# The first pair of feed-forward rows by plain products, in a one-core decoder step with Strassen products

## The reference

```python
def residual_block(x, mix, w_out_l, g_ffn, wg, wu, wd):
    x = x + mix @ w_out_l
    h = rmsnorm(x, g_ffn)
    return x + (jax.nn.silu(h @ wg) * (h @ wu)) @ wd
```

## Time and profile before

| | |
|---|---|
| median of 3 executions | 3206.66 us (3204.07 to 3212.55) |
| the profiled execution | 3213.07 us |
| its span in the trace | 3211.4 us |
| mean granted TensorE clock | 0.951 of full |
| TensorE busy | 2994.2 us |
| VectorE busy | 2013.2 us |
| ScalarE busy | 879.9 us |
| GpSimd busy | 695.3 us |
| DMA | 340.08 MB, mean 106 GB/s |

### The profile page before, as it was taken

One profiled execution on the slowest core, in us unless ns is written; L12 is line 12 of the kernel. 1 busy time (PEld: TensorE's weight loads), 2 busy tenths in 40 slices (PEclk: granted clock), 3 DMA queues, 4 the chain that ended last, 5 costly groups with the idle time before them and its releaser, 6 DMA issues.

```text
span 3211.4 us, 58867 instructions
## 1 busy us (share of the span) xinstructions
PE 2994.2 (93%) x22932; PEld 2774.9 (86%) x22932; DVE 2013.2 (63%) x3427; ACT 879.9 (27%) x1507; POOL 695.3 (22%) x774
## 2 busy tenths in 40 slices
PE   7899988999889999999989999889897999999997
PEld 6699975868789999999977999667687999999997
DVE  5798996696554444554348989865956544445444
ACT  3422123243233333300123122123323333332001
POOL 4153300001133333200041542000002333331000
PEclk9999989699899999999989999897998999999999
DMA  7354434142112222422142443352310222223222
GB/s 261 101 158 125 137 113 190 74 135 103 33 49 78 76 79 80 145 91 87 48 146 84 146 146 133 134 200 78 123 61 27 80 80 74 81 75 125 90 87 99
DMA packets 128646, 340.08 MB, mean 106 GB/s; under 512 B 20278, under 2 KB 71623, under 8 KB 123383
## 3 DMA queue, kind: packets, MB, share of 16 engines
q1 hardware_dynamic: 79426, 177.19, 15.4%
q0 software_dynamic: 33088, 102.84, 10.5%
q10 hardware_dynamic: 15844, 56.18, 5.1%
HBM read 266.10 MB, written 74.53 MB: 106 GB/s over the span
## 4 chain that ended last, share of the span: by engine, by line
PE 69%; DVE 20%; issue 4%; ACT 2%; DMA 2%; DVEq 1%; POOLq 1%; POOL 0%; SPq 0%; ACTq 0%
PE PS L1454 27%; PE PS L1476 15%; DVE U L2292 10%; PE PS L1068 7%; PE PS L1296 2%; PE PS L1403 2%; PE PS L1405 2%; PE PS L1404 2%; PE PS L1082 2%; PE PS L992 1%; PE PS L913 1%; PE PS L1014 1%; PE PS L1033 1%; DVE U L2381 1%; DVE U L2398 1%
## 5 line engine op out<-in xcount | busy, mean ns | idle before, releaser
L2292 DVE TENSOR_SCALAR_CACHE_REDUCE U<-U,smu 32x2080 bf16<-32x2080 f32 (+6 forms) x462 | 504.7, 1146 | 13.7 <-issue 1.8
L1454 PE MATMUL PS<-XAR,RGR 128*128 128x264 f32 x3168 | 404.6, 290 | 40.2 <-ACT XAR L1535 31.8
L1454 PEld LDWEIGHTS PS<-XAR,RGR 128*128 128x128 f32 x3168 | 400.9, 193 | 42.7 <-issue 33.2
L2180 DVE TENSOR_TENSOR RGR<-WS,RGR 128x512 fp32r<-128x512 f32 x308 | 238.2, 775 | 288.5 <-ACT RGR L1535 287.8
L1454 PE MATMUL PS<-XBR,RGR 128*128 128x264 f32 x2816 | 409.8, 287 | 8.5 <-DVE RGR L2180 8.5
L1454 PEld LDWEIGHTS PS<-XBR,RGR 128*128 128x128 f32 x2816 | 371.8, 190 | 8.9 <-DVE RGR L2180 8.9
L583 POOL DMA_DIRECT2D WS<-wjobs x176 | 94.6, 538 | 1191.5 <-PE PS L1476 492.3
L1535 ACT ACTIVATE U<-PS 128x528 f32<-128x528 f32 (+12 forms) x338 | 166.1, 502 | 568.6 <-PE PS L1454 253.7
L645 POOL TENSOR_TENSOR WS<-WS 128x512 f32<-128x512 f32 x176 | 257.2, 1467 | 151.7 <-DVE RGR L2180 65.3
L1535 ACT ACTIVATE RGR<-WS 128x512 fp32r<-128x512 f32 x308 | 193.0, 628 | 276.9 <-PE PS L1454 276.9
L1454 PE MATMUL PS<-HnR,RGR 128*128 128x264 f32 x1408 | 229.5, 285 | 0.0
(11 more groups left out here) (322 smaller groups left out, 5313.8 us busy)
## 6 DMA issues: line engine op xcount, KB each, us to landing
WS<-wjobs POOLq DMA_DIRECT2D x113, 512.0 KB, 3.9
WS<-wjobs ACTq DMA_DIRECT2D x50, 512.0 KB, 4.6
hmid<-U SPq DMA_DIRECT2D x44, 528.0 KB, 2.6
WS<-wjobs POOLq DMA_DIRECT2D x48, 384.0 KB, 3.3
Hn<-ckT SPq DMA_DIRECT2D x16, 896.0 KB, 10.7
Hn<-hmid SPq DMA_DIRECT2D x4, 3168.0 KB, 11.5
U<-kT_pool SPq DMA_DIRECT2D x160, 64.0 KB, 2.0
xres<-U SPq DMA_DIRECT2D x2, 4224.0 KB, 16.5
```

The lines of the kernel that those rows point to most:

```text
L1454: m = mm(out, w[:, k * P:(k + 1) * P], x[:, k, t], start=fresh and n == 0 and k == 0, stop=n == 2 and k == 3, skip_group_check=True)
L2180: tt(out=lo, in0=plain(p, i, g), in1=hi.bitcast(F32), op=ALU.subtract).then_inc(wp_lo, 1)
L2292: ts(U[0:m, JUNK[i]:JUNK[i] + w // 2].bitcast(BF16), s, CANDF[0:m, i:i + 1], None, op, ALU.add, accum_out=into[0:m, i:i + 1])
```

## The change

Pair 0 of each layer is no longer done by Strassen's scheme but by plain products; the scheme starts with pair 1.

- **TensorE:** `first_pair` takes the place of `gate_up(0)`. For each of the four weight tiles n (gate, up, gate, up) and each half of the tokens it adds up 2 (feature halves, `part`) x 2 (z) x 3 (passes) x 4 (feature blocks) = 48 matmuls of 264 columns in the two banks 2n and 2n + 1: 384 in all. The order is by what they need: the first half of the tokens, high by high on the first two blocks of b11 for tiles 0 to 2, then on the next two, tile 3, then the low weights, then the low part of b11, then b21; after that the second half of the tokens (b12, b22) by tiles 0 and 1, tile 2, tile 3.
- **Weights of pair 0:** whole tiles of 128x1024 are split at once: `row_high` (ACT; two while the last squares are formed, the third after the norm's inverse, the fourth after b11), `row_low` (DVE), which writes the low part into the tile's own slot. So a slot is in use until TensorE is done with the tile: `slot_used` for the loads of pair 1 now waits for the end of tile k on TensorE (`un_ps`, `NUNIT + 5 + k`) and not for `wp_lo`.
- **Activations:** `row_scale` works on half of the tokens at a time, the first half of the tokens first; it starts when two thirds of the inverse root are there. b11's high part is copied in two pieces. The sums t1, t2, t3 and t4 are formed by DVE alone, later in the list; t1, t3 and t4 get their high parts from ACT after the last product of `first_pair` and in the first steps of pair 1, and their low parts from `late_low` on DVE after steps 1, 3 and 5 of pair 1.
- **POOL:** the weights' sums of pair 0, `high_sums` and `high_low` go.
- **Evictions of pair 0:** four silu of 128x528 by ACT (`first_silu`) and four multiplications by DVE (`first_hidden`), straight from PSUM; the 6 snapshots and 6 additions of a Strassen pair are gone for pair 0.

The core of the diff, TensorE, POOL and the weights' side:

```diff
-                return wp_lo, W_LO + 14 * p + 11 + k
+                return (wp_lo, W_LO + 14 * p + 11 + k) if p else (un_ps, NUNIT + 5 + k)
...
+        X_ITEMS = ("b11a", "b11b", "b21", "b12", "b22", "t2", "t1", "t3", "t4")
+        X_LOWS = ("b11", "b21", "b12", "b22", "t2", "t1", "t3", "t4")
...
+        def row_hi(n):
+
+            o = (n + 2) % 3 * 1024
+            return RGR[:, o:o + 1024] if n < 3 else split_cols(XHI[3], 1024)
+
+        def row_lo(n):
+            return WSR[:, (J_GU + n) % NSLOT, 0:1024]
...
                 for p in range(NPAIR):
-                    weight_sums(L, p)
+                    if p:
+                        weight_sums(L, p)
                     for j in range(J_GU + 4 * p + 4, J_GU + 4 * p + 8):
                         load(j, job_floats(j), j - NSLOT)
...
+            def first_pair():
+
+                def products(n, half, part, w, x, ks=range(4)):
+                    hi, lo = x_part(half, part)
+                    ww, xx = (row_hi, row_lo)[w](n), (hi, lo)[x]
+                    first, last = part == 0 and w == 0 and x == 0, part == 1 and w == 1
+                    for z in range(2):
+                        for k in ks:
+                            m = mm(PS[:, 2 * n + z, 0:TQ], ww[:, (4 * part + k) * P:(4 * part + k + 1) * P],
+                                   xx[:, k, z * TQ:(z + 1) * TQ], start=first and k == 0, stop=last and k == 3,
+                                   skip_group_check=True)
+                    return m
+
+                for n, ks in ((0, (0, 1)), (1, (0, 1)), (2, (0, 1)), (0, (2, 3)), (1, (2, 3)), (2, (2, 3)),
+                              (3, (0, 1)), (3, (2, 3))):
+                    pe.wait_ge(wp_hi, row_hi_done(n))
+                    pe.wait_ge(x_hi, X_HI + ks[0] // 2 + 1)
+                    products(n, 0, 0, 0, 0, ks)
+                for n in range(4):
+                    pe.wait_ge(wp_lo, row_lo_done(n))
+                    products(n, 0, 0, 1, 0)
+                pe.wait_ge(x_lo, lo_done("b11"))
+                for n in range(4):
+                    products(n, 0, 0, 0, 1)
+                for n in range(4):
+                    pe.wait_ge(x_hi, hi_done("b21"))
+                    products(n, 0, 1, 0, 0)
+                    pe.wait_ge(x_lo, lo_done("b21"))
+                    products(n, 0, 1, 0, 1)
+                    products(n, 0, 1, 1, 0).then_inc(un_ps, 1)
+                for group in ((0, 1), (2,), (3,)):
+                    for part in range(2):
+                        for n in group:
+                            if part == 0:
+                                pe.wait_ge((f_silu, f_mul)[n % 2], n // 2 + 1)
+                            pe.wait_ge(x_hi, hi_done(("b12", "b22")[part]))
+                            products(n, 1, part, 0, 0)
+                            pe.wait_ge(x_lo, lo_done(("b12", "b22")[part]))
+                            products(n, 1, part, 0, 1)
+                            m = products(n, 1, part, 1, 0)
+                            if part:
+                                m.then_inc(un_ps, 1 if n < 3 else 7)
```

ACT's list after the squares, and DVE's `norm_split`:

```diff
                 norm_inverse(0)
-                for i in range(2):
-                    x_copy(i)
+                row_high(L, 2)
+                x_copy("b11a")
+                x_copy("b11b")
+                row_high(L, 3)
+                x_copy("b21")
                 table(ACT.Silu, 5)
-                for p in range(NPAIR):
+                x_copy("b12")
+                first_silu(0, 0)
+                x_copy("b22")
+                first_silu(0, 1)
+                x_copy("t2")
+                first_silu(1, 0)
+                weight_high(L, 14)
+                weight_high(L, 15)
+                first_silu(1, 1)
+                weight_high(L, 16)
+                x_copy("t1")
+                for p in range(1, NPAIR):
                     gates(L, p)
...
+                v.wait_ge(nrm_inv, 2)
+                for q in range(4):
+                    i = row_scale(q, 0)
+                    if q % 2:
+                        i.then_inc(fx_row, 1)
+                row_low(2)
+                low("b11", x_low(0), b11, x_high(0))
+                row_low(3)
+                for q in range(4, 8):
+                    i = row_scale(q, 0)
+                i.then_inc(fx_row, 1)
                 v.wait_ge(nrm_inv, NCH)
                 for q in range(4):
-                    i = row_scale(q)
+                    i = row_scale(q, 1)
                 i.then_inc(fx_row, 1)
...
+                low("b21", x_low(1), b21, x_high(1))
+                for q in range(4, 8):
+                    i = row_scale(q, 1)
                 i.then_inc(fx_row, 1)
...
+                low("b12", x_high(6), b12, x_high(4))
+                first_hidden(0, 0)
+                v.drain()
+                tt(out=b11, in0=b12, in1=b11, op=ALU.subtract)
                 v.drain()
                 tt(out=t2, in0=b22, in1=b11, op=ALU.subtract).then_inc(fx_sum, 1)
...
+                tt(out=b12, in0=b22, in1=b12, op=ALU.subtract).then_inc(fx_sum, 1)
+                v.wait_ge(fx_sum, 2)
+                low("b22", x_low(5), b22, x_high(5))
+                first_hidden(0, 1)
                 tt(out=b21, in0=b21, in1=t2, op=ALU.subtract).then_inc(fx_sum, 1)
...
+                low("t2", x_low(2), t2, x_high(2))
+                first_hidden(1, 0)
+                weight_low(14)
+                weight_low(15)
+                weight_low(16)
+                first_hidden(1, 1)
```

More of the change, by code:

```diff
@@ L458, in plain, with hi_done, lo_done, row_hi_done @@
                     first[:, 512:1024], second[:, 512:1024])[i]
+        X_ITEMS = ("b11a", "b11b", "b21", "b12", "b22", "t2", "t1", "t3", "t4")
+        X_LOWS = ("b11", "b21", "b12", "b22", "t2", "t1", "t3", "t4")
+        OPERAND = ("b11", "b21", "t2", "t1", "t3", "b22", "t4")
+        NX_HI, NX_LO = len(X_ITEMS), len(X_LOWS)
+        def hi_done(name):
+            return X_HI + X_ITEMS.index("b11b" if name == "b11" else name) + 1
+        def lo_done(name):
+            return X_LO + X_LOWS.index(name) + 1
+        def row_hi(n):
[3 more added lines that the diff above has]
+            return WSR[:, (J_GU + n) % NSLOT, 0:1024]
+        def row_hi_done(n):
+            return W_HI + (n + 1 if n < 3 else 14)
+        def row_lo_done(n):
+            return W_LO + (n + 1 if n < 3 else 14)
+        def x_part(half, part):
+            if half == 0:
+                return x_high(part), x_low(part)
+            return (x_high(5), x_low(5)) if part else (x_high(4), x_high(6))
         def ring(q):
@@ L1521, in _ @@
                 norm_sums(0)
-                for p in range(NPAIR):
+                first_pair()
+                for p in range(1, NPAIR):
                     gate_up(p)
@@ L2144, in norm_split @@
+                row_low(2)
[4 more added lines that the diff above has]
+                i.then_inc(fx_row, 1)
                 v.wait_ge(nrm_inv, NCH)
                 for q in range(4):
-                    i = row_scale(q)
+                    i = row_scale(q, 1)
                 i.then_inc(fx_row, 1)
-                for q in range(4, 6):
-                    row_scale(q)
-                low(0, b11)
@@ L2151, in norm_split @@
-                for q in range(6, 8):
-                    i = row_scale(q)
+                low("b21", x_low(1), b21, x_high(1))
+                for q in range(4, 8):
+                    i = row_scale(q, 1)
                 i.then_inc(fx_row, 1)
-                tt(out=b11, in0=b12, in1=b11, op=ALU.subtract).then_inc(fx_sum, 1)
-                low(1, b21)
-                weight_low(3)
+                low("b12", x_high(6), b12, x_high(4))
+                first_hidden(0, 0)
+                v.drain()
@@ L2162, in norm_split @@
-                weight_low(4)
-                low(3, b11)
-                gated(0, 2)
-                weight_low(5)
-                v.wait_ge(fx_pool, 1)
-                low(5, b22)
-                gated(0, 3)
-                weight_low(6)
-                gated(0, 4)
-                low(6, b21)
+                v.wait_ge(fx_sum, 3)
+                low("t2", x_low(2), t2, x_high(2))
[3 more added lines that the diff above has]
+                weight_low(16)
@@ L2458, in add_out @@
                     if m == KR - 2:
-                        for q in range(3):
-                            weight_low(q)
+                        for n in range(2):
+                            row_low(n)
                 gather_last(0, NCH - 1)
@@ L2740, in _ @@
                 norm_split(L)
-                for p in range(NPAIR):
+                for p in range(1, NPAIR):
                     for n in range(14):
-                        if p == 0 and n <= 4:
-                            if n == 4:
-                                weight_low(7)
-                            continue
                         gated(p, n)
                         weight_low(14 * p + n + 3)
+                        if p == 1 and n in (1, 3, 5):
```

(1 more changed line is left out.)

134 lines of the change are left out of this document (69 added, 65 removed).

## The result

| | before | after |
|---|---|---|
| median of 6 executions | 3205.82 us (3199.80 to 3212.55) | 3175.23 us (3166.86 to 3178.67) |
| profiled execution | 3213.07 us | 3177.38 us |
| its span | 3211.4 us | 3175.6 us |
| mean granted TensorE clock | 0.951 | 0.958 |

The ratio is 0.9896 with a 95% interval of 0.9885 to 0.9907: 33 us less (30 to 37), where 39.6 were forecast; the two medians of the table differ by 30.6. The change is faster, and the measured median lies in the range of 8 in 10 (3156 to 3186), but above the forecast's own (3160 to 3173); the forecast's own ratio, 3167 / 3206.7 = 0.9876, lies just outside the interval.

A forecast was written before the change was run, and what follows sets the result against it. TensorE was taken as the bound, with waits and cold clock in pair 0. Start 7.8, waits 11.6, cold spells 5.4, less 5.9 for matmuls, rest 0.9: 19.8 us per layer, 39.6 twice, giving 3167 us; 8-in-10 range 3156 to 3186.

The forecast's parts named there:

- When TensorE starts: Start of the first pair: TensorE's first matmul comes at 862.6 instead of 870.4 us.
- Whether it stays busy: Inside the first pair: every operand comes before TensorE needs it, so the pair ends at 912.2 us.
- The closest place: VectorE's low part of b22 in the first pair: ready at 893.0, wanted at 895.6, slack 2.6 us.
- The cold time: Start of the first pair: one spell of 5.4 us at half pace, costing 2.7 us; two of three spells gone.
- The pair: Output projection's end to the first pair's end: 912.2 for 932.0 us, 19.8 us less per layer.
- My split of the gain into start, waits and clock: First pair, per layer: start 7.8 us earlier, waits 11.6 and cold spells 5.4 gone, 48 matmuls 5.9 more.
- VectorE's sums: Sums on VectorE in the first pair: 2.34 us each with GpSimd idle, where the rows show 6.94 and 3.25.
- The first rival: VectorE's sums in the first pair stay long by themselves: 5.6 us per layer, 3178 us; 8 in 100.
- Whether pair 1 is ready: Behind the first pair: step 18's weights have 3.9 us of slack, late high and low parts fit; costed at nothing.
- the second rival: Pair 1's weights are late through a slow fourth load and sums: 6.8 us per layer, 3181 us; 7 in 100.
- Nothing is lost behind: Stages after the first pair: no new wait appears; the rival that nothing is gained, 3207 us, had 3 in 100.
- The slower rival: Clock stays low through the first pair's small matmul groups: 24.4 us per layer lost, 3255 us; 2 in 100.

The follow-up runs named there:

- e_more: The changed kernel with 48 more matmuls in the first pair of each layer; ratio to the kernel before 0.9936, pair 64.58 and 64.60 us.
- e_late: The changed kernel with the early start undone: VectorE waits for the inverse root's last third and scales b12 before b11; ratio to the kernel before 0.9912.
- e_warm: The changed kernel with 48 unneeded matmuls in TensorE's wait before the pair; ratio to the kernel before 0.9868, pair 56.26 and 56.24 us.
- b_half: The kernel before with only the half rows and early start, Strassen kept for pair 0; ratio to the kernel before 1.0012.
- b_dve: The kernel before with only t3 and its low part moved from GpSimd to VectorE, Strassen kept for pair 0; ratio to the kernel before 0.9976.
- e_low: The changed kernel with t1's low part moved before step 17's low weights on VectorE; ratio to the kernel before 0.9876, ten pairs 411.17 us.
- three b runs: b_half, b_dve and b_both: the kernel before with one or both parts of the change, Strassen kept for pair 0; ratios 1.0012, 0.9976 and 1.0000.
- e_best: The changed kernel with the edits of e_low and e_warm together; median 3166.53 us, ratio to the kernel before 0.9864.
- b_both: The kernel before with the edits of b_half and b_dve together, Strassen kept for pair 0; ratio to the kernel before 1.0000.

## Why the prediction was right, point by point

- **When TensorE starts.** Forecast 8.9 us after the end of the output projection (853.7 to 862.6), measured 8.9 (852.86 to 861.73). Half rows took 0.70 each and not 0.65, which cost nothing here. The norm's last third did come earlier without GpSimd's sum: the two last additions of squares took 1.17 us, not 2.38.
- **Whether it stays busy.** Right. No wait inside the pair. The closest place was the low part of b22, at 892.4; TensorE used it at about 894.6, so the slack was some 2 us for the 2.6 forecast. That what was added late in the pair counts in full (e_more) and that the start moves the end (e_late, e_warm) bear out that TensorE alone set the end.
- **The cold time.** Right: one spell, 5.5 us from the first matmul. e_warm prices it at 2.4 to 2.5 us per layer, against the 2.7 taken.
- **The pair.** Forecast 19.8 us less, measured 19.72 and 19.55. My split of the gain into start, waits and clock was an account of what stood on TensorE, not of what each edit brings: alone, the early start brought nothing (b_half), and GpSimd's relief 4.7 and 4.6 (b_dve). The parts do not add up, and the code gives a reason: with Strassen's scheme all four quarters and two sums are needed by the third product. The plain products make the early start worth something (e_late), since 192 matmuls need only the first half of the tokens.
- **VectorE's sums.** The first rival is out: t2 took 2.36 us with GpSimd idle. (One reading of the prediction was wrong, at no cost to its sum: the six whole rows that VectorE scales before b11's low part are b11, b12 and half of b21 and of b22.) b_dve (3.49 beside a sum of 1.29) and `late_low` (3.46 beside GpSimd's sums, 2.62 and 2.35 in other places) show the same exclusion. That is the rule of the Trainium skill ("SBUF — State Buffer", "Who interferes with whom"), and the traces agree with it in each of these places.
- **Whether pair 1 is ready: the step that was off.** "I cost all of this at nothing" should have been 1.33 us per layer, 2.7 in all. The two waits of 0.50 and 0.32 us delay the starts behind them by 0.7 and 0.6, because idle time is counted from the end of a matmul, and matmuls overlap: 128 of them start over 16.36 us at 911.27, where 15.7 is the full pace. It was not the late load by itself, the second rival's mechanism, but that rival came near: step 18's low weights were there with 0.5 us to spare where I had 3.9. The fourth load was issued 0.8 us after the pair's end and took 4.9 us to its sum, not 3.8, and 1.15 us lay between that sum and the one for step 18. I had taken the load of an idle queue, and this one had company: the stores of the first pair's hidden rows (528 KB each) go out at the same moments. The two stores are issued at 900.56 and about 912.6. The loads issued beside them, at 900.33 and 912.09, landed after 6.0 and 4.8 us (4.8 for the fourth in the second layer too), the other two after 3.6 and 3.7. That the stores are the cause was not tried. What set the waits in the end was VectorE's list: the low part of t1 stood ahead of step 19's low weights, ran beside GpSimd's sums and took 3.46 us. I had let VectorE's three late low parts fit "between" because each is shorter than a step, and had not placed GpSimd's sums of the same moment beside them, though the prediction itself leans on how the two engines exclude each other. e_low shows it: with the load as late as before, the move takes the 1.33 us away.
- **Nothing is lost behind.** Nearly right. From pair 2 to pair 11 nothing waits. One place stays open, TensorE's one wait in the first down products, for VectorE, which waits for a weight load: 0.7 and 1.0 us before, 1.8 and 1.9 after. In the three b runs it is 0.8 to 1.2, in e_late and e_low 1.8 to 2.0, in e_more and e_best 0.8 to 1.2, in e_warm 1.6 and 1.0. So the changed code does not force the longer wait, but four of its six traces show it and none without the change does; at most 1.9 us of the whole are at stake.
- **The number.** 39.6 us forecast; 36.6 by the stretches, 33 (30 to 37) by the times. 2.7 of the 3 us between the first two are pair 1; the rest between stretches and times is within the interval.
- **The slower rival** (the clock stays low through small groups) is out. From 869 to 911 the matmuls come in groups of 8 whose waits are already met, and the granted clock is 1.00 throughout; the groups of 4 lie in the cold spell, which ended all the same at 867.2. The second failure mode of the Trainium skill ("TensorE: Matmul & The Clock Gate", section "A second HAM failure mode: psum-queue depth-cycling") did not show in this order.

## What to carry to other kernels

A scheme that saves products can be the wrong one for the first piece, when its operands are still being made: here 14% more matmuls on data that is ready beat waiting for sums, and the reordering that feeds them was worth 2.0 us per layer without them. Account for such a stretch by where the bottleneck engine stands still, but don't read the account as a price list of the edits. And when VectorE and GpSimd both work on SBUF, place their lists side by side in time before calling either of them hidden.

## What the runs showed of the hardware that I had not expected

- In TensorE's wait of 6.3 us matmuls that nobody needs kept the granted clock at 1.00: 48 of 264 columns, 6.25 us, saved 2.4 us after it, and the pair's first matmul came no later (8.88 and 8.87 us).
- Halving VectorE's instructions along the free dimension cost little but not nothing: four of 528 elements took 2.80 us, two of 1056 took 2.53, both without a sum of GpSimd beside them. With sixteen halves instead of eight wholes (b_half, b_both) the sum t1 started 1.2 us later; part of this is GpSimd's sums, which ran beside the first eight.
- Stretches with the same code repeat to 0.1 us between the traces of different kernels, while executions of one kernel differ by 10 us (3199.80 to 3212.55 before). Differences of 1 us per layer, which the times of four to six executions cannot tell, are plain in two traces.
- Loads of 512 KB issued beside a store of 528 KB landed after 6.0 and 4.8 us, two others after 3.6 and 3.7.
